# A Fourier product ahead of a gate piece, a phase boundary without TensorE's fence, and the queries' norm ahead of the keys' low part

## Chip, cores and metric

The kernel runs on one core of one Trainium2 chip. The metric is the device time of one execution in microseconds; lower is better.

## What is computed

Four layers over 1024 tokens of width 1024, in float32: two hybrid layers (a gated recurrence and sliding-window attention), then two differential layers over 1040 tokens (16 meta tokens go in front). The change touches the differential layers alone. Cut to them, the reference is:

```python
h = rms_norm_2(h_res, norm_gain[li])
f_in, q, k, v, gate = jnp.split(h @ w_in[li], splits, axis=-1)
# Fourier half: 4 groups of 128 channels
f = jnp.fft.fft2(u, axes=(1, 3), norm="ortho").real   # along tokens and channels
f_out = jnp.einsum('blgc,gce->blge', f, w_f)
# attention half: 4 heads, two score maps c = 0, 1 per head
q = apply_partial_rotary(rms_norm_2(q, q_norm_gain[li]), cos, sin)
k = apply_partial_rotary(rms_norm_2(k, k_norm_gain[li]), cos, sin)
s = jnp.einsum('bqhcd,bkhcd->bhcqk', qb, k) * scale
a = softmax(s)[:, :, 0] - lam_f * softmax(s)[:, :, 1]
o = rms_norm_2(jnp.einsum('bhqk,bkhd->bqhd', a, vf), subln_gain[li]) * (1.0 - lambda_init)
y = jnp.concatenate([f_out, a_out], axis=-1) * jax.nn.silu(gate)
h_res = h_res + y @ w_out[li]
```

## The kernel before

One program for each engine, written out by hand in order; semaphores join them. Channels lie on the partitions, tokens along the free axis. A float32 product of full precision is made from three products of a faster format: a high part and a low part are split off each operand, and high×high, high×low and low×high are added in PSUM (`whi`, `wlo` for weights, `H[:, 0]`, `H[:, 1]` for the layer's input). Weights come by DMAs that SP issues (`tile_in`), 128 columns at a time, into two slots of `raw`; GpSimd splits them (`split_in`: one cast and four subtractions).

A differential layer (the second loop over `DEPTH`) has two phases.

**Fourier phase**, lines 1271 to 1288 on TensorE. For each of four groups, two weight tiles are projected in three pieces of tokens (348, 346, 346 columns; 24 matmuls each, L1234) into banks 0 and 1 in turn: the group's input and its gate. The Fourier transform of a group is a product along the width (`along_width`, L1250, which needs VectorE's folded input `UF`), evacuated by ScalarE as a high part `UH` (L1780) from which VectorE makes the low part `UL` (L2334), and then a product along the tokens (`along_tokens`, L1261, 60 matmuls). For group gr the order on TensorE is: width, input of group gr+1, tokens, gate of group gr+1. The last group has no input or gate to project after it, so its two products follow each other.

**Phase boundary.** The attention phase reuses the memory of the Fourier phase. Each engine drains and adds to its own phase semaphore (`end_phase`), and then waits for those of the other three (`fence`), on TensorE too, at L1290. ScalarE has behind its fence a DMA for the table of rotations, the store of group 3, a table load and an exponential (L1798 to L1802).

**Start of the attention phase.** Pieces are named by kind and number: k, q, v, g are projections (`third`, L1298), sk and sq the sums of squares over a head (L1345), vt the transposes of v. TensorE runs them in the order

```python
PRO2 = "k0 k1 k2 q0 sk q1 q2 v0 sq v1 v2 vt g0 g1 g2"
```

into banks 0 and 1 in turn; each waits until the piece two before is evacuated (`proj_free`). ScalarE evacuates (`take`, L1735), squares (L1848), and makes the inverse root from a logarithm and an exponential (L1843, L1844) in `RT`, a buffer that keys and queries share. VectorE multiplies this into the rows in four operations (`normed2`, L2363 to L2366). For the rotary part four DMAs on SP bring the partner rows to `RT` (`rotate2`, L576), and VectorE adds them in three operations (`roped2`, L2372 to L2374). Then ScalarE casts the high part into `KM` or `QH` (L1863, L1874), VectorE makes the low part (`low_keys`, L2381, in place in `QN`; `low_queries`, L2390, into `QL`), and DMAs on SP copy halves (`stack_keys`, L582; `stack_queries`, L590). Head 0 goes through this in the open, keys first; TensorE's first scores (L1358) need all of it. Every engine and SP's queue take their instructions in order.

Of the kernel before, what the change touches and what calls it, by code (L numbers as in the profile page):

```python
# [13 lines left out]
ACT = mybir.ActivationFunctionType  # L14
# [151 lines left out]
GROUPS = 4  # L166
HEADS2 = 4
HD2 = 64
CH2 = [(0, 348), (348, 346), (694, 346)]
# [32 lines left out]
def block_of(n):  # L202

    return (META + (n - 1) * P, P) if n else (0, META)
# [12 lines left out]
def step_items2(t):  # L217

    h, i = divmod(t, NB2)
    return [items2(text, h, h + 1) for text in STEPS2[h][i]] if t < NS2 else [[], []]  # L220
# [39 lines left out]
def build(nc, x, w_in, w_out, g_pre, g_post, lb_param, g_head, sinks, meta, norm_gain2, w_in2, w_fourier, q_gain2, k_gain2,  # L260
          lambda_q1, lambda_k1, lambda_q2, lambda_k2, subln_gain, w_out2, consts, lvl_mask, rope_tab, lam_tab, rope2_tab, dft, out):
    ctx = ExitStack()
    with ctx:
        def sb(name, shape, dt=F32, scope=ctx):
            return scope.enter_context(nc.sbuf_tensor(name, shape, dt))
# [85 lines left out]
        with ExitStack() as sB:  # L351
# [16 lines left out]
            GB = sb("GB", [P, 2, T2], F32, sB)  # L368
# [35 lines left out]
        g = sems.__getitem__  # L404
# [7 lines left out]
        def fence(eng, phase, but):  # L412

            for name in ("ph_act", "ph_dve", "ph_pool", "ph_pe"):
                if name != but:
                    eng.wait_ge(g(name), phase.value)

        def end_phase(eng, phase, name):
            phase.n += 1
            apart(eng)  # L420
            eng.drain().then_inc(g(name), 1)  # L421
# [45 lines left out]
        def _(sp):  # L467
# [72 lines left out]
            def load2(e, slot, L, col):  # L540
                sp.wait_ge(g("w_split"), DEPTH * W_A + e + 1)
                sp.dma_start(raw[:, slot, :].rearrange("p (t e) -> p t e", t=DT),
                             wi2[:, bass.ds(L, 1), :, bass.ds(col, P)].rearrange("p l t e -> p (l t) e")).then_inc(g(f"w_in{slot}"), 16)

            with sp.Fori(0, DEPTH) as L:
# [5 lines left out]
                def tile_in(n):  # L551

                    kind, h = TILES2[n]
                    load2(L * W_B + 2 * GROUPS + n, n % 2, L, cols2[kind] + h * P)
# [15 lines left out]
                def rotate2(kind, h):  # L570

                    m = "qk".index(kind)
                    sp.wait_ge(g("qn_ready"), L * 2 * HEADS2 + 2 * h + 2 - m)
                    for base in (0, HD2):
                        for r in (0, 8):
                            sp.dma_start(RT[base + r:base + r + 8, :], QN[base + 8 - r:base + 16 - r, m, :]).then_inc(g("rb_in"), 16)  # L576

                def stack_keys(h):

                    sp.wait_ge(g("klo_ready"), L * HEADS2 + h + 1)  # L580
                    for c in range(2):
                        sp.dma_start(KM[HD2 - HD2 * c:2 * HD2 - HD2 * c, h % 2, c, :].bitcast(F32), QN[HD2 * c:HD2 * c + HD2, 1, :]).then_inc(g("kd2_in"), 16)  # L582
# [15 lines left out]
                    tile_in(n)  # L598
                rotate2("k", 0)
                tile_in(5)  # L600
                stack_keys(0)
                rotate2("q", 0)
                stack_queries(0, 0)
                stack_queries(0, 1)
                for h in range(HEADS2 - 1):
                    if h:
                        stack_queries(h, 1)
                    n = 4 * h + 6
# [27 lines left out]
                for n in range(ST + 1):  # L636
                    a, m = block_of(n)
# [328 lines left out]
        def _(pe):  # L966
            phase = Count(None)
# [28 lines left out]
            with pe.Fori(0, DEPTH) as L:  # L996
# [160 lines left out]
                for t in range(PAIRS * 8 + 2):  # L1157
                    p, n = divmod(t, 8)
# [58 lines left out]
            with pe.Fori(0, DEPTH) as L:  # L1217
# [21 lines left out]
                def tile2(e, slot, item):  # L1239
                    for ch in range(3):  # L1240
                        project2(e, slot, item + ch, ch)

                def along_width(gr):
                    pe.wait_ge(g("fold_ready"), L * GROUPS + gr + 1)
                    if gr:
                        pe.wait_ge(g("fcat_ready"), L * GROUPS + gr)
                    for j in range(JT):
                        for m in range(2):
                            c = (j % 2) * 2 * P + m * P
                            last = nc.tensor.matmul(psum[4 + j // 2][0:JP, c:c + P], UF[:, m, j * JP:j * JP + JP], AW[:, m, gr, :], start=True, stop=True)  # L1250
                    last.then_inc(g("u1_ready"), 1)
# [28 lines left out]
                project2(1, 1, 5, 2, cols=CHF)  # L1280
                pe.wait_ge(g("awc_ready"), L + 1)
                for gr in range(GROUPS):
                    along_width(gr)
                    if gr < GROUPS - 1:
                        tile2(2 * gr + 2, 0, 6 * gr + 6)
                    along_tokens(gr)
                    if gr < GROUPS - 1:
                        tile2(2 * gr + 3, 1, 6 * gr + 9)
                end_phase(pe, phase, "ph_pe")
                fence(pe, phase, "ph_pe")  # L1290


                def third(e, slot, ch, bk):
# [91 lines left out]
                for t in range(NS2 + 2):  # L1385
                    h, i = divmod(t, NB2)
                    first, second = step_items2(t)
                    lump = lump2_of(t)
                    if i == 0 and 0 < h < HEADS2:
                        for it in first:  # L1390
                            item(*it)
                        first = []
# [59 lines left out]
        def _(act):  # L1452
            own = Count(g("act_chain"))
            link = chain(act, own)
            phase = Count(None)
# [51 lines left out]
            with act.Fori(0, DEPTH) as L:  # L1507
# [129 lines left out]
                for t in range(PAIRS * 8 + 2):  # L1637
                    p, n = divmod(t, 8)
                    if t >= 2:
                        m = (t - 2) % 8  # L1640
                        act.wait_ge(g("prt_ready"), L * PAIRS * 8 + t - 1)
                        a = P if m == 0 else 0
# [79 lines left out]
            with act.Fori(0, DEPTH) as L:  # L1722
# [11 lines left out]
                    act.wait_ge(g("proj_ready"), i0 + item + 1)  # L1734
                    nc.scalar.activation(out, (psum[odd] if bk is None else bk)[0:p, at:at + n], func, scale=scale, bias=bias).then_inc(g("proj_free"), 1)  # L1735

                def thirds(item, first, dst, func=ACT.Copy, **kw):
                    for ch, (a, n) in enumerate(CH2):
                        evac2(item + ch, (first + ch) % 2, dst[:, a:a + n], n, func, **kw)

                def first_item(item):
# [35 lines left out]
                for gr in range(GROUPS):  # L1777
                    act.wait_ge(g("u1_ready"), L * GROUPS + gr + 1)
                    for k, (j, n) in enumerate(((0, 2), (2, 2), (4, 1))):
                        nc.scalar.copy(UH[:, j:j + n, :, :].rearrange("p j m e -> p (j m e)"), psum[4 + k][0:JP, 0:n * 2 * P]).then_inc(g("uh_ready"), 1)  # L1780
                    if gr < GROUPS - 1:
                        thirds(6 * gr + 6, 0, UT[:, (gr + 1) % 2, :])
                    if gr:
                        store_group(gr - 1)
                    act.wait_ge(g("pq_ready"), L * GROUPS + gr + 1)
                    for f, (a, n) in enumerate(FCH):
                        last = nc.scalar.copy(QS[:, a:a + n], psum[6 + f][:, 0:n])
                    last.then_inc(g("qs_ready"), 1)
                    if gr < GROUPS - 1:
                        if gr:  # L1790
                            act.wait_ge(g("cat_out"), (L * (CT2 - 1) + gr) * 16)
                        thirds(6 * gr + 9, 1, GB[:, (gr + 1) % 2, :], ACT.Silu)
                end_phase(act, phase, "ph_act")


# [90 lines left out]
                for it in items2(PRO2, 0, 0):  # L1886
                    if it == ("v", 0, 1):
                        high_keys(0)
                    if it == ("g", 0, 2):
                        high_queries(0, 0)  # L1890
                        high_queries(0, 1)
                    take(*it)
                gate_silu(0)
                for t in range(NS2 + 2):
                    h, i = divmod(t, NB2)
                    first, second = step_items2(t)
# [81 lines left out]
        def _(dve):  # L1978
# [11 lines left out]
            phase = Count(None)  # L1990
# [70 lines left out]
            with dve.Fori(0, DEPTH) as L:  # L2061
# [139 lines left out]
                for t in range(PAIRS * 8 + 1):  # L2201
                    p, n = divmod(t, 8)
# [91 lines left out]
            with dve.Fori(0, DEPTH) as L:  # L2294
# [64 lines left out]
                def normed2(kind, h):  # L2359

                    m = "qk".index(kind)
                    dve.wait_ge(g("rx_ready"), L * 2 * HEADS2 + 2 * h + 2 - m)
                    link(V.scalar_tensor_tensor(SQ[:, :], SQ[:, :], -0.5, RT[:, :], ALU.mult, ALU.mult))  # L2363
                    link(V.tensor_tensor(SQ[:, :], SQ[:, :], RT[:, :], ALU.mult))
                    link(V.scalar_tensor_tensor(SQ[:, :], SQ[:, :], 1.5, RT[:, :], ALU.add, ALU.mult))
                    V.scalar_tensor_tensor(QN[:, m, :], QN[:, m, :], qkg[:, m:m + 1], SQ[:, :], ALU.mult, ALU.mult).then_inc(g("qn_ready"), 1)  # L2366

                def roped2(kind):

                    m = "qk".index(kind)  # L2370
                    dve.wait_ge(g("rb_in"), (L * 2 * HEADS2 + 2 - m) * 64)
                    V.tensor_tensor(QN[:, m, :], QN[:, m, :], rope2[:, 0, :], ALU.mult)  # L2372
                    link(V.tensor_tensor(RT[:, :], RT[:, :], rope2[:, 1, :], ALU.mult))
                    V.tensor_tensor(QN[:, m, :], QN[:, m, :], RT[:, :], ALU.add).then_inc(g("rp_ready"), 1)  # L2374

                def low_keys(h):

                    dve.wait_ge(g("khi_ready"), L * HEADS2 + h + 1)
                    for c in range(2):
                        r = slice(HD2 * c, HD2 * c + HD2)  # L2380
                        last = V.tensor_tensor(QN[r, 1, :].bitcast(F32R), QN[r, 1, :], KM[r, h % 2, c, :].bitcast(F32), ALU.subtract)  # L2381
                    last.then_inc(g("klo_ready"), 1)
# [50 lines left out]

                normed2("k", 0)
                roped2("k")
                low_keys(0)
                normed2("q", 0)
                roped2("q")
                low_queries(0, 0)
                low_queries(0, 1)  # L2440
# [47 lines left out]
                for n in range(EARLY2, ST + 1):  # L2488
                    a, m = block_of(n)
# [45 lines left out]
```

## Time and profile before

| | |
|---|---|
| runs | 3633.98, 3633.2, 3638.49 us |
| median | 3633.98 us |
| profiled execution | 3641.37 us |
| span of its instructions | 3639.6 us |
| TensorE busy | 3386.5 us (93%) |
| VectorE busy | 2055.7 us (56%) |
| ScalarE busy | 1570.7 us (43%) |
| GpSimd busy | 1461.6 us (40%) |
| mean granted clock of TensorE | 0.973 of full speed |

In the rows below PE is TensorE, PEld its weight loads, DVE VectorE, ACT ScalarE, POOL GpSimd, and SP the engine that only issues DMAs; q behind a name means its instruction queue (DVEq, SPq). L numbers are lines of the kernel. A bracket at the end of a row of a timeline gives the idle time of the engine just before and what ended it. `f32` stands for the faster format too. The names of buffers are given without numbers, and a tile that shares memory with others can show under their common name: `SR` is the pair of `SQ` and `RT`. The first differential layer lies between some 2110 and 2950 us of the span, the second behind it.

### The profile page before, as it was taken

To read this page: it belongs to the slowest core of one execution; us is meant where nothing else is said; L and a number is where in the kernel's file an instruction comes from. 1 tells how busy PE (TensorE), PEld (TensorE's weight loads), DVE (VectorE), ACT (ScalarE), POOL (GpSimd) and SP (SyncE) were. 2 spreads that over 40 slices of the span, in tenths; PEclk is the share of its full clock that TensorE was granted. 3 is DMA by queue.
4 is the path that set the end of the run, shared out by engine and by line. 5 is a ranking of instruction groups with operands and counts; after the bars stand their busy time and mean duration, and the time that the engine had idled before them with its cause. 6 is when DMAs were issued, how large, how long until landed. Compare 5 with 4: busy or idle time off the path is not lost.

```text
span 3639.6 us, 59943 instructions
## 1 busy us (share of the span) xinstructions
PE 3386.5 (93%) x18080; PEld 2745.7 (75%) x18080; DVE 2055.7 (56%) x5230; ACT 1570.7 (43%) x3221; POOL 1461.6 (40%) x1830
## 2 busy tenths in 40 slices
PE   8999999998999999999998999889888999889878
PEld 6888886665878888886666789777775798677756
DVE  5666665666266666666674362376553323665543
ACT  6454443443255444534443351355552322555532
POOL 6565554333515655554334322233242122323341
PEclk9999999998999999999998999999998999999989
DMA  5111112111221111121111231210121512111124
GB/s 147 36 36 29 35 29 65 44 38 42 93 88 44 36 30 35 35 54 45 36 39 62 87 104 47 68 31 24 44 78 45 160 54 62 33 39 37 47 69 144
DMA packets 217950, 206.47 MB, mean 57 GB/s; under 512 B 17948, under 2 KB 185260, under 8 KB 216668
## 3 DMA queue, kind: packets, MB, share of 16 engines
q1 hardware_dynamic: 197536, 137.80, 13.5%
q0 software_dynamic: 12208, 47.03, 3.7%
q10 hardware_dynamic: 7920, 18.19, 1.6%
q8 instruction: 136, 2.23, 0.3%
q14 instruction: 150, 1.23, 0.1%
HBM read 148.04 MB, written 37.01 MB: 51 GB/s over the span
## 4 chain that ended last, share of the span: by engine, by line
PE 72%; DVE 11%; issue 8%; ACT 6%; DMA 1%; DVEq 1%; ACTq 1%; POOL 0%; SPq 0%; POOLq 0%
PE banks L1013 24%; PE banks L1298 7%; PE banks L1182 5%; PE banks L1234 5%; PE banks L1316 4%; PE banks L1206 4%; PE banks L1380 4%; PE banks L1128 2%; PE banks L1371 2%; PE banks L1261 2%; PE banks L1138 2%; PE banks L1150 2%; PE banks L1051 2%; DVE BB L2085 1%; DVE SM L2237 1%
## 5 line engine op out<-in xcount | busy, mean ns | idle before, releaser
L1013 PE MATMUL banks<-H,whi 128*128 128x512 f32 x3200 | 1046.5, 408 | 5.6 <-ACT VT L1518 3.9
L1013 PEld LDWEIGHTS banks<-H,whi 128*128 128x128 f32 x3200 | 572.8, 188 | 184.9 <-issue 65.7
L1013 PE MATMUL banks<-H,wlo 128*128 128x512 f32 x1600 | 632.2, 395 | 0.0
L667 POOL CAST whi<-raw 128x1024 fp32r<-128x1024 f32 x150 | 165.4, 1103 | 968.1 <-PE banks L1013 383.7
L670 POOL TENSOR_TENSOR wlo<-raw,whi 128x256 fp32r<-128x256 f32 (+1 forms) x246 | 406.1, 1666 | 12.1
L1298 PE MATMUL banks<-H,whi 128*128 128x346 f32 (+1 forms) x1536 | 386.2, 335 | 9.9 <-DVEq L421 8.0
L2399 DVE TENSOR_SCALAR_CACHE_REDUCE SP<-banks 128x346 f32<-128x346 f32 (+3 forms) x432 | 202.1, 513 | 280.0 <-PE banks L1359 278.2
L1013 PEld LDWEIGHTS banks<-H,wlo 128*128 128x128 f32 x1600 | 301.8, 189 | 69.3
L1298 PEld LDWEIGHTS banks<-H,whi 128*128 128x128 f32 x1536 | 276.4, 196 | 17.4 <-issue 14.0
L1660 ACT ACTIVATE SM<-SM,stt 128x256 f32<-128x256 f32 (+1 forms) x256 | 124.7, 488 | 323.1 <-DVE stt L2242 323.1
L1298 PE MATMUL banks<-H,wlo 128*128 128x346 f32 (+1 forms) x768 | 253.1, 330 | 0.0
L2108 DVE TENSOR_TENSOR EX<-EX,QB 128x128 f32<-128x128 f32 (+1 forms) x448 | 241.7, 563 | 2.3 <-issue 0.3
L2221 DVE TENSOR_TENSOR SM<-banks,cst 128x512 f32<-128x512 f32 (+1 forms) x128 | 84.2, 658 | 193.6 <-PE banks L1128 193.6
L1358 PE MATMUL banks<-KM,QH 128*128 128x346 f32 (+3 forms) x432 | 161.4, 376 | 29.7 <-DMA QH<-QH 19.3
L1234 PE MATMUL banks<-H,whi 128*128 128x346 f32 (+3 forms) x768 | 183.5, 324 | 3.2 <-DVE H L2038 2.0
L1371 PE MATMUL banks<-cst,SP 128*128 128x128 f32 (+3 forms) x648 | 99.3, 291 | 80.2 <-DVE SP L2409 50.5
L1930 ACT ACTIVATE SP<-SP,st 128x1040 f32<-128x1040 f32 x144 | 166.3, 1159 | 15.0 <-DVE st L2464 14.7
L1182 PE MATMUL banks<-H,CHI 128*128 128x512 f32 x512 | 164.7, 403 | 8.0 <-DVE CLO L2253 8.0
L1206 PE MATMUL banks<-H,CHI 128*128 128x512 f32 x512 | 162.4, 398 | 1.5 <-DVE CLO L2253 1.5
L2118 DVE COPY AT<-banks 32x32 f32<-32x32 f32 (+1 forms) x384 | 76.4, 199 | 147.1 <-PE banks L1058 122.6
L670 POOL TENSOR_TENSOR H<-raw,H 128x256 fp32r<-128x256 f32 (+2 forms) x128 | 149.3, 1181 | 19.7 <-POOL H L667 18.1
L2108 DVE TENSOR_TENSOR EX<-EX,KB 128x128 f32<-128x128 f32 (+1 forms) x448 | 153.4, 368 | 2.0
(311 smaller groups left out, 7372.5 us busy)
## 6 DMA issues: line engine op xcount, KB each, us to landing
raw<-in_w_in SPq DMA_DIRECT2D x148, 512.0 KB, 3.9
raw<-in_w_out SPq DMA_DIRECT2D x64, 256.0 KB, 2.6
XT<-x_resident POOLq DMA_DIRECT2D x18, 512.0 KB, 4.0
x_resident<-XT POOLq DMA_DIRECT2D x18, 512.0 KB, 2.9
raw<-in_w_out SPq DMA_DIRECT2D x18, 512.0 KB, 5.1
RQ<-QR SPq DMA_DIRECT2D x112, 64.0 KB, 2.0
XB<-x_resident POOLq DMA_DIRECT2D x14, 512.0 KB, 4.8
SR<-cat_resident SPq DMA_DIRECT2D x16, 448.0 KB, 4.3
```

Of the source, the lines that this page charges most:

```text
L667: link(nc.gpsimd.tensor_copy(hi, src))
L670: last = nc.gpsimd.tensor_tensor(lo[:, a:a + n], src[:, a:a + n], hi[:, a:a + n].bitcast(F32), ALU.subtract)
L1013: last = nc.tensor.matmul(bank(half if bk is None else bk), w[:, slot, k, :], H[:, part, a:a + 512], start=k == 0 and n == 0, stop=k == DT ...
L1182: last = nc.tensor.matmul(bank(s), c[:, t % 2, s, :], H[:, part, t * 512:t * 512 + 512], start=t == 0 and n == 0, stop=t == CT - 1 and n == 2)
L1206: last = nc.tensor.matmul(bank(s), c[:, th, t % 8, :], H[:, part, t * 512:t * 512 + 512], start=t == 0 and n == 0, stop=t == CT - 1 and n ...
L1234: last = nc.tensor.matmul(psum[item % 2][:, 0:n], w[:, slot, k, :], H[:, part, k * T2 + a:k * T2 + a + n], start=k == 0 and m == 0, stop=k ...
L1298: last = nc.tensor.matmul(bk[:, 0:n], w[:, slot, k, :], H[:, part, k * T2 + a:k * T2 + a + n], start=k == 0 and m == 0, stop=k == DT - 1 a ...
L1358: nc.tensor.matmul(bk, QH[:, c, q0:q0 + nq], KM[:, h % 2, c, a:a + n], start=True, stop=False)
L1371: last = nc.tensor.transpose(psum[5 + (3 * t + n) % 2][0:m, at * P:at * P + nq], SP[0:nq, t % 2, 0, a:a + m], ident[0:nq, 0:nq])
L1930: last = nc.scalar.activation(SP[0:nq, t % 2, c, :], SP[0:nq, t % 2, c, :], ACT.Exp, scale=-1.0, bias=st[:, 8 + c:9 + c], accum_out=st[:, ...
L2108: return V.tensor_tensor(e, e, x, ALU.mult)
L2399: V.tensor_scalar(SP[0:nq, t % 2, c, a:a + n], psum[2 + k % 3][0:nq, 0:n], -1.0, None, ALU.mult, ALU.min, accum_out=st2[0:nq, t % 2, 3 * c ...
```

## The change

Three things, all in the differential layer.

1. The last group's product along the width now stands between the second and the third piece of its own gate, instead of behind the third. ScalarE's evacuation of that third piece moves behind its three casts of `UH`.
2. `fence` is no longer called for TensorE between the phases. `end_phase` stays, and the other engines' fences stay.
3. For head 0, VectorE norms the queries before it makes the keys' low part; SP issues the queries' rotation before the copies of the keys; ScalarE casts the queries' high part before it evacuates g1 instead of before g2.

```diff
@@ sync
                 rotate2("k", 0)
                 tile_in(5)
+                rotate2("q", 0)
                 stack_keys(0)
-                rotate2("q", 0)
                 stack_queries(0, 0)
                 stack_queries(0, 1)
@@ tensor
                 for gr in range(GROUPS):
-                    along_width(gr)
                     if gr < GROUPS - 1:
+                        along_width(gr)
                         tile2(2 * gr + 2, 0, 6 * gr + 6)
                     along_tokens(gr)
                     if gr < GROUPS - 1:
-                        tile2(2 * gr + 3, 1, 6 * gr + 9)
+                        for ch in range(3):
+                            if (gr, ch) == (GROUPS - 2, 2):
+                                along_width(GROUPS - 1)
+                            project2(2 * gr + 3, 1, 6 * gr + 9 + ch, ch)
                 end_phase(pe, phase, "ph_pe")
-                fence(pe, phase, "ph_pe")
@@ scalar
-                def thirds(item, first, dst, func=ACT.Copy, **kw):
-                    for ch, (a, n) in enumerate(CH2):
+                def thirds(item, first, dst, func=ACT.Copy, chunks=range(3), **kw):
+                    for ch in chunks:
+                        a, n = CH2[ch]
                         evac2(item + ch, (first + ch) % 2, dst[:, a:a + n], n, func, **kw)
...
                     if gr < GROUPS - 1:
                         thirds(6 * gr + 6, 0, UT[:, (gr + 1) % 2, :])
+                    else:
+                        thirds(6 * gr + 3, 1, GB[:, gr % 2, :], ACT.Silu, chunks=[2])
...
-                        thirds(6 * gr + 9, 1, GB[:, (gr + 1) % 2, :], ACT.Silu)
+                        thirds(6 * gr + 9, 1, GB[:, (gr + 1) % 2, :], ACT.Silu, chunks=range(3 if gr < GROUPS - 2 else 2))
...
-                    if it == ("g", 0, 2):
+                    if it == ("g", 0, 1):
                         high_queries(0, 0)
                         high_queries(0, 1)
@@ vector
                 normed2("k", 0)
                 roped2("k")
+                normed2("q", 0)
                 low_keys(0)
-                normed2("q", 0)
                 roped2("q")
```

On TensorE, from the last gate piece of group 3 (L1234, input `H`) to the start of the tokens' product (L1261, inputs `UH`, `UL` and the tables `TH`, `TL`), before:

```order
L1234 MATMUL banks<-H,whi 128x346 x2
L1234 MATMUL banks<-H,wlo 128x346
L1244 ISA
L1246 ISA
L1250 MATMUL banks<-AW,UF 105x128 x10
L1254 ISA
L1261 MATMUL banks<-TH,UH 128x262
```

and with the change:

```order
L1234 MATMUL banks<-H,wlo 128x346
L1244 ISA
L1246 ISA
L1250 MATMUL banks<-AW,UF 105x128 x10
L1224 ISA
L1225 ISA
L1234 MATMUL banks<-H,whi 128x346 x2
...
L1234 MATMUL banks<-H,wlo 128x346
L1254 ISA
L1261 MATMUL banks<-TH,UH 128x262
```

The width product (L1250) and its two waits (L1244, L1246) moved ahead of a whole gate piece; the wait for `UL` (L1254) now stands behind that piece.

Again on TensorE, from the end of the tokens' product of group 3 to the first key piece (L1298), the difference's lines of before:

```order
-L416 REGISTER_ALU x3
-L1324 ISA
-L1294 ISA
-L1298 MATMUL banks<-H,whi 128x348 x2
```

and the changed kernel there:

```order
L1261 MATMUL banks<-TH,UL 128x260
L1326 ISA
L1296 ISA
L1300 MATMUL banks<-H,whi 128x348 x2
```

The three register operations with the fence's waits (L416) are gone; the waits for the bank and for the weights (now L1326 and L1296) stay.

On VectorE, head 0, from the rotated keys to the rotated queries, before:

```order
L2374 TENSOR_TENSOR QN<-QN,SR 128x1040
L2378 ISA
L2381 TENSOR_TENSOR QN<-QN,KM 64x1040 x2
L2362 ISA
L2363 SCALAR_TENSOR_TENSOR SR<-SR 128x1040
...
L2366 SCALAR_TENSOR_TENSOR QN<-QN,qkg,SR 128x1040
L2371 ISA
L2372 TENSOR_TENSOR QN<-QN,rope 128x1040
```

and with the change (line numbers are five higher):

```order
L2379 TENSOR_TENSOR QN<-QN,SR 128x1040
L2367 ISA
L2368 SCALAR_TENSOR_TENSOR SR<-SR 128x1040
...
L2371 SCALAR_TENSOR_TENSOR QN<-QN,qkg,SR 128x1040
L2383 ISA
L2386 TENSOR_TENSOR QN<-QN,KM 64x1040 x2
L2376 ISA
L2377 TENSOR_TENSOR QN<-QN,rope 128x1040
```

The four operations of the norm moved ahead of the keys' low part, which now stands between the norm and the wait for the queries' rotation.

## Rows read from the trace of the kernel before

**Rows 1.** The page: busy time of each engine; the chain that ended last.
```profile
PE 3386.5 (93%) x18080; PEld 2745.7 (75%) x18080; DVE 2055.7 (56%) x5230; ACT 1570.7 (43%) x3221; POOL 1461.6 (40%) x1830
...
PE 72%; DVE 11%; issue 8%; ACT 6%; DMA 1%; DVEq 1%; ACTq 1%; POOL 0%; SPq 0%; POOLq 0%
```

**Rows 2.** Waits of TensorE, whole span: us in total, times, longest.
```profile
PE banks L1358 <- DMA QH<-QH: 19.3, 2, 9.7
...
PE banks L1298 <- DVEq L421: 8.0, 2, 4.0
...
PE banks L1261 <- DVE UL L2334: 4.7, 2, 2.3
```

**Rows 3.** The chain in order of time: start, us, what; last from layer 2.
```profile
2260.09 7.33 PE banks L1261 x60
2267.42 11.46 PE banks L1234 x72
2278.88 2.20 PE banks L1250 x20
...
2283.39 9.09 PE banks L1261 x60
...
2296.47 17.07 PE banks L1298 x96
...
3039.10 18.02 PE banks L1298 x96
```

**Rows 4.** Windows: length, TensorE busy (instructions), granted clock, DMA share, GB/s.
```profile
2283.30:2287.00 3.70, 3.61 (x17) 0.54 0.49 147
...
2296.40:2300.50 4.10, 4.03 (x16) 0.58 0.72 183
...
3104.80:3108.50 3.70, 3.61 (x12) 0.50 1.00 274
```

**Rows 5.** Timeline, layer 1, end of the fold and end of ScalarE's boundary work.
```profile
2272.20 0.16 DVE L2326 COPY UF<-UT 128x2 f32<-128x2 f32 x1
...
2298.58 0.20 ACT L1802 ACTIVATE lsum<-lsum 128x2 f32<-128x2 f32 x1
```

**Rows 6.** Timeline, layer 1, from the keys' norm to the first scores.
```profile
2318.61 1.24 DVE L2363 SCALAR_TENSOR_TENSOR SR<-SR 128x1040 f32<-128x1040 f32 x1 [13.02 <-ACT SR L1844]
...
2333.08 1.07 ACT L1844 ACTIVATE SR<-SR 128x1040 f32<-128x1040 f32 x1
...
2336.21 2.48 DVE L2381 TENSOR_TENSOR QN<-QN,KM 64x1040 fp32r<-64x1040 f32 x2 [4.26 <-ACT KM L1863]
2338.72 1.96 DVE L2363 SCALAR_TENSOR_TENSOR SR<-SR 128x1040 f32<-128x1040 f32 x1
...
2344.11 1.66 DVE L2366 SCALAR_TENSOR_TENSOR QN<-QN,qkg,SR 128x1040 f32<-128x1040 f32 x1
...
2347.93 0.46 ACT L1735 ACTIVATE GB<-banks 128x346 f32<-128x346 f32 x1 [3.35 <-PE banks L1298]
...
2350.31 1.24 DVE L2372 TENSOR_TENSOR QN<-QN,rope 128x1040 f32<-128x1040 f32 x1 [4.54 <-DMA SR<-QN]
...
2352.74 1.96 DVE L2374 TENSOR_TENSOR QN<-QN,SR 128x1040 f32<-128x1040 f32 x1
...
2356.85 2.84 SPq L590 DMA_DIRECT2D QH<-QH  x4
...
2361.37 0.65 PE L1358 MATMUL banks<-KM,QH 128*128 128x348 f32 x1 [9.67 <-DMA QH<-QH]
```

**Rows 7.** Timeline of GpSimd, layer 1: parts of a split alone, then two later splits.
```profile
2311.12 2.81 POOL L670 TENSOR_TENSOR wlo<-raw,whi 128x256 fp32r<-128x256 f32 x4
...
2337.81 1.78 POOL L667 CAST whi<-raw 128x1024 fp32r<-128x1024 f32 x1 [9.97 <-PE banks L1298]
2339.67 6.69 POOL L670 TENSOR_TENSOR wlo<-raw,whi 128x256 fp32r<-128x256 f32 x4
2351.98 1.62 POOL L667 CAST whi<-raw 128x1024 fp32r<-128x1024 f32 x1 [5.62 <-PE banks L1298]
```

## The prediction

> **What bounds the kernel.** I read the page first, for the share of each engine [rows 1]: TensorE is busy for 93% of the span and carries 72% of the chain that ended last, so time goes away where TensorE idles or is slow, and hardly elsewhere. Next the list of waits on TensorE, to find which idle times the change touches [rows 2]: the first row is what TensorE idles for in front of the scores (one very long wait per layer), the second a wait in front of the first product of the attention phase, the third one in front of the product along the tokens; each comes twice, once per layer. Then the chain in order of time [rows 3], which gives whole stretches of matmuls and so the price of a stretch with a stall in front of it against the same work without one. Then windows with the granted clock [rows 4], and last the timeline around the three places [rows 5 to 7]. All of it is the differential layer, which runs twice, so each term counts twice.
>
> The sum is made against the profiled execution, 3641.37 us. The median of the three runs shown is 3633.98 us, 7.4 us or 0.2% lower; I take the difference found in the trace off the median. About 0.2% (7.3 us) is also what a measurement of this kernel can tell from no change.
>
> **Part 1: last group's first product ahead of a gate piece.** It adds no instruction. In the layer of [rows 3] the three gate pieces take 11.46 us for 72 matmuls, 3.82 us apiece; then comes the product along the width, 2.20 us; then TensorE idles 2.33 us until VectorE has the low parts [rows 2], and only then runs the 60 matmuls along the tokens. The change puts the last gate piece between the two. Its 3.82 us cover the high parts (ScalarE) and low parts (VectorE), which by the wait itself end 2.33 us behind the width product. So the 2.33 us go. Is the width product ready 3.8 us sooner? It needs VectorE's fold, whose last instruction ends at 2272.36 [rows 5]; the second piece ends at 2278.88 − 3.82 = 2275.06. There are 2.7 us to spare. Gain 2.33 us per layer.
>
> The stall costs more than its length. The same 60 matmuls take 7.33 us in the group before and 9.09 us behind the stall [rows 3], and the granted clock over the first 3.7 us of them is 0.54, the lower level of 1.2 GHz for nearly all of that [rows 4]. In front of it TensorE had run at full clock and then idled. Without the idle time I expect 7.33 us: 1.76 us more per layer.
>
> Moved with it: on ScalarE three casts stand ahead of the evacuation of gate piece 3 instead of behind it, and the store of group 2 behind both. ScalarE waits for gate pieces anyway (3.35 us in front of one [rows 6]), so this costs nothing; without that cover it would be the casts, which fit into the 2.33 us. GpSimd's split of the first query tile waits for the last gate piece, now 2.2 us later; its parts take 2.81 us [rows 7], and between lie the tokens' product and three key pieces, 18.8 us.
>
> **Part 2: no fence for TensorE.** TensorE still drains and reports, so ScalarE and VectorE wait as before; it no longer waits for them. Now it idles 4.01 us [rows 2] behind the tokens' product and the next 96 matmuls (k0, k1, k2, q0) take 17.07 us in the first layer, 18.02 us in the second [rows 3], against 4 × 3.82 = 15.28 us; the clock of the first 4.1 us is 0.58 [rows 4]. So the low clock costs 1.79 and 2.74 us.
>
> What is late next? The key pieces alternate between two banks, and the third needs the first one evacuated. ScalarE's first evacuation stands behind its own fence, two DMA issues, a table load and an exponential that ends at 2298.78 [rows 5]. From the end of the tokens' product (2283.39 + 9.09 = 2292.48) that is 6.3 us; with 0.46 us for the evacuation bank 0 is free 6.8 us after it. TensorE would need it after 0.3 + 2 × 3.82 = 7.9 us. Margin 1.1 us: two products hide the whole fence. What remains of the 4.01 us is the drain, which the trace never shows by itself. Bounds: 0 if it overlaps, and 0.65 us, the length of a first matmul behind a wait [rows 6]. I take 0.3, the middle, as no row is near it. [...] Gain 3.71 + 1.79 = 5.50 us, and 3.71 + 2.74 = 6.45 us.
>
> The key and query chain behind hangs on the evacuated k2, hence on TensorE, and moves forward with it: VectorE waits 13.02 us for ScalarE in front of the first keys' norm [rows 6], so the clears it does there have room.
>
> **Part 3: the queries' norm ahead of the keys' low part.** Clock times here are those of before; parts 1 and 2 shift all alike. TensorE idles 9.67 us for the copied halves of QH [rows 6]. The chain up to there: ScalarE ends the queries' root factor at 2334.15, but VectorE first waits for KM and does the keys' low part (2336.21 to 2338.69), then the norm, 2338.72 to 2345.77. Then the four rotation DMAs, 4.54 us; the rotation, 2350.31 to 2354.70; ScalarE's QH; the copy; scores at 2361.37.
>
> - Start: the norm can begin 0.05 us after the factor, as the keys' did. 2338.72 − 2334.20 = 4.52 us.
> - Length: the keys' norm has ops of 1.24 us, the queries' 1.96 and three of about 1.67 [rows 6], because GpSimd splits a weight tile beside them: its cast takes 1.78 us, and its four parts 6.69 us against 2.81 us when alone [rows 7]. The split hangs on a TensorE product and starts at 2337.81 still. Three of the four ops of the moved norm are then over; the fourth meets the cast, about 2 us. End about 2340.0: 5.8 instead of 7.05 us, 1.25 us gained.
> - The keys' low part moves under the split: 2 × 1.67 from 2340.0, end 2343.4. The rotation's DMAs land at 2340.0 + 4.54 = 2344.6, so it stays hidden, by 1.2 us. That is what is late next here.
> - The rotation then falls after the split: three ops of 1.24, 3.7 instead of 4.39 us, 0.7 us gained, end 2348.3. Next split at 2351.98 [rows 7].
> - ScalarE casts QH from 2348.3. This now stands ahead of gate piece 1, ready at 2347.93 [rows 6], which is held up for about 3 us (2.15 us from the rotated queries to the first issue of QH's copy [rows 6], and a short second part); TensorE needs that bank only after the first scores. On SP the four rotation issues stand ahead of the KM copies, which start at 2343.4, 4.7 us later than now; given the rotation's 4.54 us they land at 2348, 7 us before the scores.
>
> Sum 4.52 + 1.25 + 0.7 = 6.4 us per layer, and an idle of about 3.3 us stays in front of the scores. Bounds: 4.5 (all as slow as now) and 7.2 (all four ops at 1.24 us). I take a value between, since the split's start falls inside the norm. The Trainium skill (SBUF — State Buffer, Who interferes with whom) calls the shared port an exclusive lock, the later of the two fully blocked. By that rule an op beside a split part takes 1.24 + 0.70 = 1.94 us; the trace has this for the first op, and 1.67 for the others, so the measurement decides. By the rule the sum would be 0.2 us worse over both layers.
>
> **Sum.** Layer 1: 2.33 + 1.76 + 5.50 + 6.4 = 16.0 us. Layer 2: 2.33 + 1.77 + 6.45 + 6.4 = 16.95 us. Together 32.9 us: 3608.5 us for the profiled execution, **3601 us** for the median.
>
> **Rivals.**
> - A, only parts 1 and 2 pay, and the scores still wait for something the norm doesn't move (KM copies behind the rotation on SP, or the low part sticking out over the rotation's landing). For: several links now have margins of about 1 us. Against: the QH row names the last releaser, and KM landed long before. Gain 20.1 us: 3614 us. Chance 0.08.
> - B, the wait of the fence comes back at the third key piece, since ScalarE's evacuation is later than reckoned, and part 2 pays half (some 6 us). Gain 27 us: 3607 us. The margin is 1.1 us. Chance 0.10.
> - C, the idle time in front of the scores, shortened to 3.3 us, no longer brings the clock down. The 3.7 us window behind it is at 0.50 [rows 4], so 1.85 us per layer would come on top: 3597 us. Against: in both layers 2.33 us were enough in part 1. The Trainium skill (TensorE: Matmul & The Clock Gate, What's actually happening) has the clock fall through idleness and rise through activity; by it a shorter gap can be spared. Chance 0.12.
> - D, slower: VectorE and ScalarE are queues in order, and both now have query work ahead of work ready sooner (the keys' low part; gate piece 1). If the queries' factor came late, everything waits for it. Each us by which the rotated queries come later than now, relative to TensorE, costs 2 us in all, from −20.1 us; slower by over 7.3 us from 13.7 us late. At 15 us it gives 3644 us. The factor is an output of ScalarE behind a TensorE sum, both in an unchanged place, so this would need something unseen. Chance 0.03.
> - E, no effect: the stalls only change place, ScalarE or GpSimd being the true bound at 43% and 40% busy. 3634 us. Chance 0.03.
>
> **Numbers.** Forecast 0.64, A 0.08, B 0.10, C 0.12, D 0.03, E 0.03. The forecast's own range is 28.5 to 34.5 us gained, 3599.5 to 3605.5 us. Taking in A, B and C and the spread of the runs: 3594 to 3615 us. Faster 0.94, same 0.03, slower 0.03.
>
> **What would show it.** In the profile after: no idle in front of the tokens' product in the last group; 60 matmuls in 7.3 us; k0 within half a us of them, at full clock, with no wait at the third key piece; VectorE's second norm right behind ScalarE's factor; the keys' low part inside the rotation's wait; about 3.3 us in front of the scores, released by QH. A wait of TensorE for ScalarE's evacuation of a key piece would speak for B, one for KM or QL for A, full clock at the first scores for C. A gain under 19 us would mean that the chain behind k2 did not move with TensorE, and that I am wrong.

## The result, and the profile after

The changed kernel takes 3607.64 us (median of 4 runs, 3604.2 to 3609.17) against 3633.59 us (median of 4, 3630.97 to 3638.49): 26 us less, a ratio of 0.9923 with a 95% interval of 0.9911 to 0.9936. A second set of runs gave 3609.19 us and 0.9927 (0.9914 to 0.9941). The prediction was 3601 us, in a range of 3594 to 3615. The gain was put at 32.9 us and is 26: the idle times went as forecast, the clock did not give back what was put down for it. The time lies in the wide range that took in the rivals, but outside the forecast's own 3599.5 to 3605.5 us.

The waits of TensorE after, whole span (us in total, times, longest), against [rows 2]:

```profile
PE banks L1360 <- DMA QH<-QH: 6.2, 2, 3.1
```

The waits for `UL` and for the fence (4.7 and 8.0 us in [rows 2]) have no row any more. The wait for QH is 6.2 instead of 19.3 us, and still has the same releaser.

The chain after in order of time (start, us, what), layer 1, against [rows 3]:

```profile
2253.58 7.33 PE banks L1261 x60
2260.90 7.64 PE banks L1234 x48
2268.54 2.18 PE banks L1250 x20
2270.72 3.81 PE banks L1234 x24
2274.54 7.32 PE banks L1261 x60
2281.86 0.34 issue
2282.20 7.89 PE banks L1300 x48
2290.11 7.90 PE banks L1300 x48
```

Everything joins. The width product is followed by the last gate piece, that by the tokens' product of 7.32 us (9.09 before), then 0.34 us (the 4.01 us of before), then the 96 matmuls k0 to q0. They end 15.8 us after they began (17.07 before). The chain shows them as two rows, split where the third key piece begins; why is told under the third key piece of part 2 below.

The clock right there (windows: length, TensorE busy, granted clock, DMA share, GB/s), against 0.54 and 0.58 in [rows 4]; the last two are the first 3.7 us behind the scores' wait, in layer 1 and in layer 2:

```profile
2277.00:2281.80 4.80, 4.80 (x40) 1.00 0.33 99
2282.20:2286.30 4.10, 4.10 (x26) 1.00 0.00 0
2339.20:2342.90 3.70, 3.62 (x23) 1.00 0.53 154
3066.60:3070.30 3.70, 3.68 (x23) 1.00 0.57 165
```

And the queries' chain, timelines of VectorE, ScalarE, GpSimd, SP and TensorE after, layer 1, against [rows 6] and [rows 7]:

```profile
2317.56 1.07 ACT L1849 ACTIVATE SR<-SR 128x1040 f32<-128x1040 f32 x1
2318.66 1.24 DVE L2368 SCALAR_TENSOR_TENSOR SR<-SR 128x1040 f32<-128x1040 f32 x1 [2.24 <-ACT SR L1849]
...
2322.28 1.07 POOL L667 CAST whi<-raw 128x1024 fp32r<-128x1024 f32 x1 [9.97 <-PE banks L1300]
2322.50 1.96 DVE L2371 SCALAR_TENSOR_TENSOR QN<-QN,qkg,SR 128x1040 f32<-128x1040 f32 x1
...
2324.38 3.46 DVE L2386 TENSOR_TENSOR QN<-QN,KM 64x1040 fp32r<-64x1040 f32 x2
2324.48 2.65 SPq L576 DMA_DIRECT2D SR<-QN  x4
...
2328.90 1.32 DVE L2377 TENSOR_TENSOR QN<-QN,rope 128x1040 f32<-128x1040 f32 x1 [1.06 <-DMA SR<-QN]
...
2332.69 2.55 ACT L1879 CAST QH<-QN 64x1024 fp32r<-64x1024 f32 x4 [3.65 <-DVE QN L2379]
...
2339.28 0.42 PE L1360 MATMUL banks<-KM,QH 128*128 128x348 f32 x1 [3.10 <-DMA QH<-QH]
```

The norm starts 0.03 us behind ScalarE's factor. Three of its operations run alone, the fourth meets GpSimd's split (the cast and the first subtraction) and takes 1.96 us; the keys' low part (3.46 us) lies inside the wait for the rotation and leaves 1.06 us of it. TensorE idles 3.10 us.

### The profile page after: what moved, and what is told of

Read it like the earlier page. It is cut to its first block, busy times and chain, and to the rows that moved or that the text cites. A ratio compares the mean times of both kernels' runs of the same rounds, so it can differ in the third digit from the quotient of the medians.

```text
span 3602.4 us, 59937 instructions
## 1 busy us (share of the span) xinstructions
PE 3376.1 (94%) x18080; PEld 2737.1 (76%) x18080; DVE 2051.4 (57%) x5230; ACT 1570.2 (44%) x3221; POOL 1455.4 (40%) x1830
## 4 chain that ended last, share of the span: by engine, by line
PE 72%; DVE 10%; issue 8%; ACT 5%; DMA 2%; DVEq 1%; POOL 0%; ACTq 0%; SPq 0%; POOLq 0%
PE banks L1013 24%; PE banks L1300 7%; PE banks L1182 5%; PE banks L1234 5%; PE banks L1206 4%; PE banks L1382 4%; PE banks L1318 3%; PE banks L1128 2%; PE banks L1373 2%; PE banks L1138 2%; PE banks L1261 2%; PE banks L1051 2%; PE banks L1150 2%; DVE BB L2090 1%; DVE SM L2242 1%
## 5 line engine op out<-in xcount | busy, mean ns | idle before, releaser
L1234 PE MATMUL banks<-H,whi 128*128 128x346 f32 (+3 forms) x768 | 183.7, 324 | 3.2 <-DVE H L2043 2.0
L1373 PE MATMUL banks<-cst,SP 128*128 128x128 f32 (+3 forms) x648 | 99.5, 291 | 80.7 <-DVE SP L2414 50.9
```

Of the source, the lines that this page charges most:

```text
L1234: last = nc.tensor.matmul(psum[item % 2][:, 0:n], w[:, slot, k, :], H[:, part, k * T2 + a:k * T2 + a + n], start=k == 0 and m == 0, stop=k ...
L1373: last = nc.tensor.transpose(psum[5 + (3 * t + n) % 2][0:m, at * P:at * P + nq], SP[0:nq, t % 2, 0, a:a + m], ident[0:nq, 0:nq])
```

## The experiments

The forecast had two kinds of terms: idle time that goes (25 us over both layers) and half clock that goes with it (8.1 us). 26 us look like the first alone. Two theories were set against each other. A stall here is a stretch in which TensorE is idle; half clock is the lower of its two levels, a granted clock of 0.50. **P**: a stall of this kernel has its stretch of half clock as a fixed part, so every term should be found again, and the 26 us are chance. **C**: only the idle time is sure; whether and where the clock falls changes from one execution to the next. Single-execution figures of the differential layers below are the span less the start of the first product of the first differential layer (L1234); the recurrent layers ahead are the same program in all kernels, and yet that start lay anywhere from 2144.9 to 2154.5 us.

**The kernel before, once more.** No edit.

> The kernel before, unchanged, for a second profile. Theory P (path): the six stalls come again at the same lengths (2.33, 4.01, 9.67 us in each layer), each followed by about 3.5 us at half clock, so the low-clock terms of 1.8 to 2.7 us are a fixed part of each stall. Theory C (clock elsewhere): the idle times come again to 0.1 us, but at least one of the stretches behind them runs at full clock in this profile, or is low by another length; the low clock is then not a fixed price of a stall. Ratio to before 1.000 within 0.001 under both.

Measured: 3635.23 us, ratio 0.9998 (0.9989 to 1.0007). One kernel alone spreads widely: from 3627.46 to 3641.54 us in the 27 runs of before that this ratio and the next three rest on. The idle times came again as 2.33, 4.01, 9.73 us and 2.33, 4.01, 9.65 us. The clock behind them (windows as above, one behind each of the first two stalls of layer 1, then the first and the last of layer 2):

```profile
2281.69:2285.40 3.71, 3.71 (x30) 1.00 0.48 141
2293.24:2297.34 4.10, 4.10 (x14) 0.50 0.76 205
3025.30:3029.00 3.70, 3.70 (x30) 1.00 0.51 142
3102.40:3106.10 3.70, 3.67 (x13) 0.50 1.02 274
```

The stall of 2.33 us is followed by full clock here, in both layers, where the profile behind the prediction had 0.54 in the same place [rows 4]. So its 1.76 us are not a fixed price of the stall. The two longer stalls have half clock again. So P fails for the short stall and holds for the long ones.

**The changed kernel, once more.** No edit.

> The changed kernel, unchanged, for a second profile and more rounds. Theory P: the gain is 33 us (ratio 0.991) and the 26 us measured were short because of few runs. Theory C: the gain stays at 25 to 28 us (ratio 0.9925), since only the idle time taken out (2 x 12.5 us) is sure; the profile shows low clock behind later waits of the attention phase at other places than the first profile of this kernel did.

Measured: 3609.19 us, 0.9927. The idle in front of the scores is 3.12 and 3.08 us; behind it the clock was full in both layers of the first profile, and here:

```profile
2338.47:2342.17 3.70, 3.70 (x23) 1.00 0.54 156
3064.65:3068.35 3.70, 3.70 (x13) 0.50 0.56 162
```

Full in layer 1, half in layer 2, with the same idle time to 0.04 us. The differential layers took 1456.8 and 1456.1 us in the two profiles, against 1487.5 and 1486.3 us for before: 30.4 us less, of which 25.1 us are idle time. I summed the time lost to the lower clock over them (busy time of TensorE times one less the granted clock, in windows of 2 us): 57.5 and 58.4 us before, 51.5 and 53.5 us after, so 5.5 us less, not 8.1. The timed runs give 26 us. The profiled executions flatter the change: those of before took 3641.37 and 3638.53 us, above their medians, and those of after 3604.2 and 3602.96 us, each the fastest of its set. C's number for the total came out; its claim that lower clock returns at other places is only partly borne out, since some of it did go.

**Part 1 alone.**

```diff
-                    along_width(gr)
                     if gr < GROUPS - 1:
+                        along_width(gr)
...
+                            if (gr, ch) == (GROUPS - 2, 2):
+                                along_width(GROUPS - 1)
```

ScalarE's evacuation of the third gate piece moves with it, as in the change.

> Part 1 alone. Theory P: the idle time of 2.33 us and the half clock behind it (1.76 us) go in both layers, 8.2 us faster (ratio 0.9977). Theory C: 4.7 us for the idle time is sure, the clock part comes and goes, so 4.7 us (0.9987).

Measured: 3629.66 us, 0.9984 (0.9974 to 0.9994), 5.6 us less. The stall for `UL` is gone, the others are untouched (4.01, 9.61 us). Both theories' numbers, 8.2 and 4.7 us, lie in the interval of 2.2 to 9.5 us, so this time cannot tell them apart; for this stall the second profile of before does.

**Part 2 alone.**

```diff
                 end_phase(pe, phase, "ph_pe")
-                fence(pe, phase, "ph_pe")
```

> Part 2 alone, with the stall of 2.33 us still there. Theory P: 3.7 us of idle time and 1.8 and 2.7 us of half clock go, 11.9 us faster (0.9967). Theory C: 7.4 us (0.998). A rival for both, that the third key piece waits for ScalarE: a wait of TensorE for the first evacuated key piece up to 0.5 us.

Measured: 3627.43 us, 0.998 (0.9971 to 0.9989), 7.9 us less: C's 7.4 rather than P's 11.9, which lies just outside the interval of 4 to 10.5 us. Yet the 4.01 us stall was followed by half clock in all eight places where profiles of this case have it (two layers each in the profiles of before, before again, part 1 alone and part 3 alone). The half clock of this stall is gone from the profile of this kernel, but the low clock of the whole span hardly is. Each timed run has its mean granted clock on record, to 0.001; one less that clock, times the span, averages 93.6 us over the 11 runs of this kernel and 93.9 us over the 27 of before, each average good to about 1 us. (It counts low clock under idle time too.) So low clock came back elsewhere. The profile shows one place, behind a wait of 1.79 us for VectorE in layer 2; the first two windows are of this kernel, the last two, behind the same wait, of part 1 alone:

```profile
3159.10:3161.10 2.00, 2.00 (x6) 0.50 0.00 0
3161.10:3163.10 2.00, 2.00 (x6) 0.72 0.00 0
3160.40:3162.40 2.00, 1.99 (x15) 1.00 0.00 0
3162.40:3164.40 2.00, 2.00 (x8) 1.00 0.00 0
```

No wait of TensorE for an evacuated key piece shows in its list.

**Part 3 alone.** The three moves of the diff on SP, ScalarE and VectorE.

> Part 3 alone. Both theories: the idle time in front of the scores falls from 9.67 to about 3.2 us in each layer, 13 us faster (ratio 0.9964). If the clock behind it stays up now (idle of 3.1 us was followed by full clock three times of four), up to 17 us (0.9953).

Measured: 3620.61 us, 0.9955 (0.994 to 0.9969), 15.6 us less, between both numbers. The idle in front of the scores, from the list of waits:

```profile
PE banks L1298 <- DVEq L421: 8.0, 2, 4.0
PE banks L1358 <- DMA QH<-QH: 6.2, 2, 3.1
PE banks L1261 <- DVE UL L2334: 4.7, 2, 2.3
```

The same 3.1 us as in the changed kernel, with both other stalls in place: as to idle time the parts do not disturb each other. Behind the shortened wait the clock was low in both layers (0.54 and 0.55 over 3.7 us). Their gains measured alone, 5.6 + 7.9 + 15.6 = 29 us, are as good as the whole, 26 us, within their intervals.

**Parts 1 and 2 without 3** (what rival A says would pay).

> Parts 1 and 2 without part 3 (rival A of the prediction: only these pay). Theory P: 20.1 us faster (0.9945). Theory C: the idle times alone, 2 x (2.33 + 3.67) = 12.0 us (0.9967). The profile shows 9.6 to 9.7 us in front of the scores, as before.

Measured: 3622.11 us, 0.9961 (0.9947 to 0.9975), 14.1 us less. C's 12.0 us lie in the interval, P's 20.1 us lie just outside it. The wait for QH is 9.60 and 9.65 us, so everything behind the third key piece moves as one with TensorE and the wait itself does not grow.

**SP's order undone.** The changed kernel, but

```diff
-                rotate2("q", 0)
                 stack_keys(0)
+                rotate2("q", 0)
```

> The changed kernel with one piece of part 3 undone: on SP the copies of the keys are issued ahead of the queries' rotation again, while VectorE norms the queries first. The rotation is then held in SP's queue until the keys' low part is done (3.5 us) and the two copies are issued (1.2 us): idle time in front of the scores 3.1 + 4.7 = 7.8 us, 9.4 us slower than the changed kernel (ratio to before 0.9952). If SP's order does not matter, as the changed kernel.

Measured: 3614.58 us, 0.9939 (0.9925 to 0.9952), 5.4 us above the changed kernel's 3609.19, where 9.4 was expected, a ratio of 0.9952 at the edge of the interval. In the profile the differential layers took 1466.4 us, 9.6 and 10.3 us more than in the two profiles of the changed kernel. Idle time in front of the scores 7.97 and 7.91 us, where 7.8 was expected. SP's queue and VectorE there:

```profile
2330.39 1.18 SPq L582 DMA_DIRECT2D KM<-QN  x2
2331.71 2.89 SPq L576 DMA_DIRECT2D SR<-QN  x4
```

```profile
2325.02 1.96 DVE L2371 SCALAR_TENSOR_TENSOR QN<-QN,qkg,SR 128x1040 f32<-128x1040 f32 x1
2326.91 3.46 DVE L2386 TENSOR_TENSOR QN<-QN,KM 64x1040 fp32r<-64x1040 f32 x2
2336.36 1.24 DVE L2377 TENSOR_TENSOR QN<-QN,rope 128x1040 f32<-128x1040 f32 x1 [5.99 <-DMA SR<-QN]
```

The norm ends at 2326.98, but the rotation is issued 4.73 us later, behind the key copies that wait for the low part. In idle time the queue's order is worth 4.8 of part 3's 6.5 us per layer. In timed runs it is 5.4 us of some 13 (3622.11 us without part 3, 3609.19 with it); why less than the 9.6 us of idle time is open.

**ScalarE's cast back behind gate piece 1.** The changed kernel, but

```diff
-                    if it == ("g", 0, 1):
+                    if it == ("g", 0, 2):
                         high_queries(0, 0)
```

> The changed kernel with ScalarE's cast of QH behind the evacuation of gate piece 1 again, its place before the change. In the changed kernel the rotated queries are ready 0.6 us or so after that piece's product, so the cast would start at most 0.5 us later: idle time in front of the scores 3.1 to 3.6 us, within 1 us of the changed kernel (ratio to before 0.993). If the place of the cast carries the gain of part 3, the idle time goes back towards 9.7 us and the kernel is 6 us or more slower.

Measured: 3607.46 us, 0.9931 (0.9917 to 0.9944), the changed kernel's time, as expected. ScalarE's timeline there, layer 1:

```profile
2334.95 0.46 ACT L1737 ACTIVATE GB<-banks 128x346 f32<-128x346 f32 x1 [3.35 <-PE banks L1300]
2335.44 2.55 ACT L1879 CAST QH<-QN 64x1024 fp32r<-64x1024 f32 x4
```

The cast follows the evacuation at once, and TensorE idles 3.31 instead of 3.10 us. This piece of the change buys 0.2 us of idle time per layer, which timed runs cannot show.

**One step further.** What was left is an idle TensorE of 3.1 us in front of the scores, waiting for a DMA. Steps of later heads run the next head's first key piece ahead of the scores; head 0 did not:

```diff
-                    if i == 0 and 0 < h < HEADS2:
+                    if i == 0 and h < HEADS2:
                         for it in first:
                             item(*it)
                         first = []
```

> The changed kernel with one more step: the first key piece of head 1 (24 matmuls, 3.82 us) stands ahead of the first scores of head 0 instead of between their halves. If the 3.1 us of idle time in front of the scores are only a wait for the copied QH, the piece covers them: no wait for QH, 6.2 us faster than the changed kernel (ratio to before 0.991). If the piece's own weights or its bank are late, TensorE waits there for GpSimd or ScalarE instead, and nothing is won.

Measured: 3597.4 us, 0.9894 (0.9879 to 0.9909). The same kernel again:

> The same kernel as early_key, for more rounds. Theory C: the idle time of 3.1 us per layer is gone for sure (6.2 us below the changed kernel), the clock behind the scores' start, which was low in one of four profiles of the changed kernel's stall, adds up to 2 us: 3600 to 3603 us if the first look was lucky, 3597 us if it was not. No wait for QH in the profile.

Measured: 3597.88 us, 0.9903 (0.9888 to 0.9918), the second of the two guesses. Both intervals lie below the changed kernel's 0.9923 and 0.9927; the medians are about 10 us lower (9.6 us below the late cast's kernel, which ran beside the second). TensorE's timeline around the first scores, layer 1:

```profile
2338.41 0.48 PE L1300 MATMUL banks<-H,whi 128*128 128x348 f32 x2
2338.73 0.32 PE L1300 MATMUL banks<-H,wlo 128*128 128x348 f32 x1
2338.89 0.33 PE L1360 MATMUL banks<-KM,QH 128*128 128x348 f32 x1
2339.05 0.32 PE L1361 MATMUL banks<-KM,QL 128*128 128x348 f32 x1
```

No idle time, full clock (matmuls of 348 columns 0.16 us apart). The piece of 3.82 us covers the wait, and the list of waits has no row for QH. 6.2 us of the 10 are the idle time. The clock behind the first scores was 1.00 in both layers of both profiles, where the changed kernel had 0.50 in one place of four. Over the whole span, the low clock of the timed runs (reckoned as for part 2) is 79.1 us in these 8 runs and 84.5 in 9 of the changed kernel, so part of the rest is clock; how much of it belongs to this place is not shown.

## Why the prediction was right, and where it was off

- **Part 1, the idle time: right.** 2.33 us went in both layers, the fold was in time, and nothing took its place.
- **Part 1, the clock: mis-sized.** The step "the stall costs more than its length ... 1.76 us more per layer" took one execution's low clock for a property of the stall. The profiles hold this stall eight times (before, before again, part 2 alone, part 3 alone, two layers each), and six of them are followed by a clock of 1.00 over the next 4 us; the other two are those of the forecast's profile. By these eight the term is some 0.9 us for both layers, an estimate (a quarter of 3.5).
- **Part 2, the idle time: right, what is left of it misread.** 4.01 became 0.34 us in both layers; 0.3 was taken, as the middle of two bounds. The prediction gives it to the drain and says that the trace never shows the drain by itself. It does: in layer 1 of before TensorE's DRAIN (L421) ends at 2292.51, 0.05 us behind the last matmul, and with the change at 2281.91, again 0.05 us behind. The rest are the waits for the bank and for the weights, 0.1 us apart, and the step to the first weight load.
- **Part 2, the third key piece: right by a hair.** The margin of 1.1 us was gone in layer 1, and the piece began 0.18 us late. ScalarE ended its boundary work 7.8 us after the tokens' product instead of 6.3, since the issue of one store took 1.77 instead of 0.33 us:

```profile
2286.34 1.77 ACTq L1761 DMA_DIRECT2D cat_resident<-GB  x1
2288.13 1.28 ACT L1805 ACT_TABLE_LOAD   x1 [5.58 <-issue]
2289.43 0.20 ACT L1807 ACTIVATE lsum<-lsum 128x2 f32<-128x2 f32 x1
```

  In layer 2 it took 0.33 us as before. Rival B was near, then; it stayed at 0.18 us because two products cover 7.9 us. The time measured, 3607.6 us, is the one that the prediction gives for rival B (3607), yet the cause was not B's: 0.18 us in one layer is all that the third key piece cost, and what was missing is clock.
- **Part 2, the clock: mis-sized.** Half clock behind this stall is in every profile that has the stall, and cost 1.79 and 2.74 us in the forecast's profile. Taking the stall away gave 7.9 us in timed runs, little more than its 7.3 us of idle time. The step that failed is the one from "low clock stands behind the stall" to "without the stall it is saved": the low clock of the whole span stayed the same, 93.6 against 93.9 us. A small part was never clock: the 96 matmuls take 15.5 us at full clock behind the drain, not the 15.28 us of the forecast, 0.25 us per layer. Where else it came back is shown for one later wait only.
- **Part 3: right.** Forecast 6.4 us per layer and 3.3 us of idle left; measured 6.5 and 3.1. The norm took 5.8 us as put; the low part 3.46 instead of 3.34 us; the rotation landed 1.06 us behind it, forecast 1.2. The 0.2 us by which the sum would be worse if every operation beside a part of the split took 1.94 us stands there without working; the one operation of the norm that met the split took 1.96 us.
- **Rival C came true half the time.** Behind the shortened wait, of 3.1 to 3.3 us, the clock was full in four and lower in four of the eight places (the changed kernel twice, part 3 alone, the late cast). In the changed kernel itself it was full in three of four, and still the time is not C's 3597 us.
- **Rivals A, D and E did not happen.** No new row in TensorE's list of waits took the removed time.

Sum: idle time 25.1 us, forecast 24.9; clock 8.1 forecast, 5.5 by the profiles, about 1 by the timed medians. The last two differ by 4 us. A cause at hand is the choice of executions: both profiled ones of after were the fastest of their sets, both of before slower than their medians. It is not shown to be all of it. That the time fell within the range at all is owed in part to its width: the range had to cover A, B and C, and the forecast's own was missed by 2 us.

## What to carry to other kernels

Price a stall by its idle time, which repeats to 0.1 us between executions, and put the low clock behind it into the range and not into the forecast. A second profile shows whether it is there at all; even where every profile had it (the stall of 4.01 us), taking the stall away gave little more than the idle time. When work is reordered on one engine, look at the order of the DMA queue that serves it: here it decided 4.8 us of idle time per layer, and the reordered cast beside it 0.2. A phase fence is needed by the engines that write into reused memory; one whose banks and inputs are already guarded by their own semaphores can run ahead as far as its banks allow, here two products. And where an engine waits for a transfer, look for a piece already behind it in the order that needs nothing of it.

## What the hardware showed unasked

- The clock after the same idle time differs between executions of one program: after 2.33 us it was 0.57 and 0.69 (over 4 us) in one profile of before and 1.00 and 1.00 in the next; after 3.1 us it was 1.00 three times and 0.50 once in two profiles of the changed kernel; after 4.01, 7.9 and 9.6 us in the places of this document it was low all 20 times (0.50 to 0.63). The length of the wait alone does not tell: behind waits of 1.97 us for VectorE later in the layer (L1371, L1373 after), which follow other waits closely, it was 0.50 to 0.63 every time, in all twelve profiles.
- The issue of the same store behind the fence took ScalarE 0.33 us in both layers of before and in layer 2 of the changed kernel, but 1.77 us in layer 1 of its first profile, and 0.33 again there in the second. Four more of the layers without TensorE's fence show 1.24 to 1.57 us: part 2 alone (layer 2), parts 1 and 2, the late cast and the first early-key profile (layer 1). That makes 5 of 16 layers without the fence and none of the 8 with it. Nothing in these runs says why.
